# Attention over head pairs: the values product at full array width, and three pauses moved by one or two k-tiles

## The chip, the cores and the metric

The kernel runs on one core of one Trainium2 chip, in one launch. The time is device microseconds of that core. Before the change it is 2374.72 us, the median of three runs (2372.66 to 2375.34). All inputs and the output are float32.

## The reference, cut to what matters

The reference is a chain of two blocks over x of 512 tokens by 2048 features. The change lies in the attention of the first block: sliding-window attention with 32 query heads of 64 features, 4 key/value heads, ALiBi slopes and a sink column.

```
def swa_sink_mixer(h, w_in, sinks):
    q, k, v, z = jnp.split(h @ w_in, [BRANCH, BRANCH + KV_A, BRANCH + 2 * KV_A], axis=-1)
    ...                                   # q: 4 blocks x 128 tokens x 4 kv heads x 8 heads x 64
    kb, vb = band(k), band(v)             # each block of keys with the one before it
    scores = jnp.einsum('bnqhgd,bnkhd->bnhgqk', q, kb) * (HEAD_DIM ** -0.5)
    scores = scores - slopes[:, :, None, None] * dist
    scores = jnp.where(valid[None, :, None, None], scores, NEG)
    p = jax.nn.softmax(jnp.concatenate([scores, sink_col], axis=-1), axis=-1)[..., :-1]
    o = jnp.einsum('bnhgqk,bnkhd->bnqhgd', p, vb).reshape(B, S, BRANCH)
    return o, z
# then y = (o * silu(z)) @ w_out ; x = x + rmsnorm(y)
# second block, two layers: rmsnorm, projections, latent attention, gated convolution,
# attention over 256 memory tokens, gate, output projection, residual
```

## The kernel before

Features lie on the partitions and the 512 tokens on the free axis. A weight chunk is 128 output columns, 1 MB, 16 k-tiles of 128x128. To keep float32 accuracy a weight and an activation are each split in two parts (`hi`, `lo`), and a k-tile is three matmuls of 512 columns (hi·hi, hi·lo, lo·hi), all at line 444 (`passes`, called by `features`). One chunk is thus 48 matmuls. ScalarE makes `hi` (line 748), VectorE `lo` (line 1054).

The first block's attention goes over 16 pairs of heads (`PAIRS`), numbered from 0; both heads of a pair share one key/value head. A pair has two chunks: the query chunk (`chunk1(PAIR1, i)`) and the gate chunk (`chunk1(PAIR1 + 1, i)`). The attention of a pair is laid between k-tiles: `features` takes a list `meanwhile` of (pause, step), and a step runs ahead of the k-tile with the number of its pause. The steps are, on TensorE:

- `scores_first(i)` (lines 519, 520) in the gate chunk of pair i: 16 matmuls of 256 columns into the four banks of `sc`. It waits for `q_split`, the two halves of the query, and for the keys of the pair (`kcur_done`, copies by GpSimd at lines 382 and 386).
- `turn_first(i)` (line 531) in the query chunk of pair i+1: 14 transposes of 128x128 blocks of probabilities. It waits for `probs1`.
- `values_first(i)` (line 543) between the query and the gate chunk of pair i+1: 8 matmuls of the turned probabilities `pt1` (the moving operand, 256 columns, or 128 for the last key block) against the values `vcur` (the stationary operand). It waits for the turned tiles (copied by ScalarE at line 809 and VectorE at line 1193), for `vcur` (GpSimd, line 393) and for the reader of the pair before.

`vcur` holds for each of four key blocks 128 columns: the same 64 value columns twice, once for each head of the pair. Before, the head `par` uses columns `par * 64` on, writes partitions `par * 64` on of the bank `ov[par]`, and the two heads alternate matmul by matmul. The reader (`y_first`, line 1187) takes 64 partitions of each bank.

The query halves that scores wait for are made after the end of the query chunk: VectorE scales the chunk out of PSUM (line 1197, `dg`), ScalarE copies the upper part (line 815), VectorE subtracts (line 1201, two instructions, named `q<-dg,q`), which releases `q_split`. The order on VectorE in one pair is: split of the gate chunk, copies of the turned tiles (1193), scaling (1197), subtraction (1201), `y_first` of the pair before (1187), split of the next query chunk (1054), softmax (1161 to 1178), gate (1207, 1209). Each engine runs its queue in order; a semaphore holds back the instruction that waits and all behind it.

Pair 0 stands alone, pairs 1 to 13 are a hardware loop, and pairs 14 (`A`) and 15 (`B`) are written out behind it: `q_a`, values(13), `q_b` (which is the query chunk of pair 15) with scores(14), `z_a` with turn(14) and the last scores, values(14), `z_b` with turn(15), values(15). Then the activations are split (lines 762 and 1225) and the first block's output product starts.

Of the kernel before, what the change touches and what calls it, by code (L numbers as in the profile page):

```python
# [22 lines left out]
def build(nc, xT, memT, mem, pos, gains, sinks, consts, window, w1, w2, wm, out):  # L23
# [11 lines left out]
    P = 128  # L35
    D, S, MEM = 2048, 512, 256
    KT, TB, MB = D // P, S // P, MEM // P
# [5 lines left out]
    HD, PAIRS, KVH = 64, 16, 4  # L43
    HALVES = (slice(0, HD), slice(HD, 2 * HD))
    PAIR1 = 4
# [32 lines left out]
    def chunk1(p, i=0):  # L78

        new = isinstance(i, int) and i == 0 and p < 2  # L80
        return Chunk(i * 2 + p, p % 2, i + p // 2, None if new else 2)
# [14 lines left out]
    A, B = PAIRS - 2, PAIRS - 1  # L96
    q_a, q_b, z_a, z_b = chunk1(PAIR1, A), chunk1(PAIR1 + 1, A), chunk1(PAIR1, B), chunk1(PAIR1 + 1, B)
# [26 lines left out]
    with ctx:  # L124
        free = [(nc.sbuf_base + 63) // 64 * 64]

        def sb(name, cols, dt=F32, at=None):

            if at is None:
                at = free[0]  # L130
                free[0] += (cols * 4 + 63) // 64 * 64
            return nc.alloc_sbuf_tensor_at(name, [P, cols], dt, offset=at)
# [4 lines left out]
        h_hi, h_lo = sb("h_hi", KT * S, F32R), sb("h_lo", KT * S, F32R)  # L137
# [13 lines left out]
        zt = sb("zt", S, at=free[0])  # L151
# [7 lines left out]
        prob1, pt1 = sb("prob1", 2048, at=m0), sb("pt1", 2048, at=m0 + 8192)  # L159
# [17 lines left out]
        vcur, q1 = sb("vcur", 512, at=a0 + 5120), sb("q1", 2 * S, F32R, at=a0 + 7168)  # L177
# [18 lines left out]
        ov = [ctx.enter_context(nc.psum_tensor(f"ov{s}", [P, 512], F32)) for s in range(2)]  # L196
        sc = ctx.enter_context(nc.psum_tensor("sc", [P, 2048], F32))

        def bank(b, n=512, off=0):
            return sc[:, 512 * b + off:512 * b + off + n]  # L200

        def tile(t, n=S):

            return slice(t * n, (t + 1) * n) if isinstance(t, int) else bass.ds(t * n, n)
# [229 lines left out]
        def _(pe):  # L434
            def begin(c):
                pe.wait_ge(lo_done, c.n + 1)
                if c.back is not None:
                    pe.wait_ge(evacuated[c.slot], c.uses)
# [8 lines left out]
            def k_tile(c, k, x_hi, x_lo, first, last):  # L447
                w, x = tile(k, P), tile(k)
                return passes(acc[c.slot][:, :], hi[c.slot][:, w], lo[c.slot][:, w], x_hi[:, x], x_lo[:, x], first, last)

            def features(c, x_hi, x_lo, ready=None, meanwhile=()):

                begin(c)
                for k in range(KT):
                    for pause, other in meanwhile:
                        if k == pause:
                            other()
                    if ready is not None:
                        ready(k)
                    ins = k_tile(c, k, x_hi, x_lo, k == 0, k == KT - 1)  # L460
                ins.then_inc(chunk_done, 1)
# [37 lines left out]
            def spread(no, to, n=S, diag=dg):  # L499

                pe.wait_ge(diag_done, no + 1)
                pe.matmul(to, ones, diag[:, 0:n], start=True, stop=True).then_inc(r_done, 1)
# [9 lines left out]
            def scores_first(i):  # L512
                pe.wait_ge(q_split, i + 1)
                pe.wait_ge(kcur_done, i * 3 + 3)
                for b in range(TB):
                    for par in range(2):
                        to = bank(2 * par + b // 2, 256, b % 2 * 256)
                        q, k = tile(par * TB + b, P), slice(b * P, b * P + 256)
                        pe.matmul(to, q1[:, q], k_hi[:, k], start=True, stop=False)  # L519
                        ins = pe.matmul(to, q1[:, q], k_lo[:, k], start=False, stop=True)  # L520
                ins.then_inc(scores1, 1)

            def turn_first(i):
                pe.wait_ge(probs1, i + 1)
                for kb in range(TB):
                    for par in range(2):
                        for nxt in range(2):
                            b = kb + nxt
                            if b < TB:
                                src = par * 1024 + b * 256 + (1 - nxt) * P  # L530
                                ins = pe.transpose(bank(kb, P, par * 256 + nxt * P), prob1[:, src:src + P], ident)  # L531
                ins.then_inc(turned1, 1)

            def values_first(i):
                pe.wait_ge(pt1_act, i * 2 + 2)
                pe.wait_ge(pt1_dve, i * 2 + 2)
                pe.wait_ge(vcur_done, i * 2 + 2)
                pe.wait_ge(y1, i + 1)
                for kb in range(TB):
                    n = 256 if kb < TB - 1 else P  # L540
                    for par, rows_ in enumerate(HALVES):
                        src = kb * 512 + par * 256
                        ins = pe.matmul(ov[par][rows_, kb * P:kb * P + n], vcur[:, kb * P + par * HD:kb * P + (par + 1) * HD],  # L543
                                        pt1[:, src:src + n], start=kb == 0, stop=kb == TB - 1, skip_group_check=True)
                ins.then_inc(values1, 1)

            def pair(i, first):

                features(chunk1(PAIR1, i), h_hi, h_lo,
                         meanwhile=[(9, (lambda: spread(1, ov[1][:, 0:MEM], MEM, zt)) if first else lambda: turn_first(i - 1))])  # L550
                if not first:
                    values_first(i - 1)
                features(chunk1(PAIR1 + 1, i), h_hi, h_lo, meanwhile=[(4 if first else 3, lambda: scores_first(i))])

            def last_scores():
                pe.wait_ge(pt1_act, A * 2 + 2)
                pe.wait_ge(pt1_dve, A * 2 + 2)
                scores_first(B)

            pair(0, True)  # L560
            with pe.Fori(1, A) as i:
                pair(i, False)
            features(q_a, h_hi, h_lo, meanwhile=[(9, lambda: turn_first(A - 1))])
            values_first(A - 1)
            features(q_b, h_hi, h_lo, meanwhile=[(3, lambda: scores_first(A))])
            features(z_a, h_hi, h_lo, meanwhile=[(8, lambda: turn_first(A)), (12, last_scores)])
            values_first(A)
            features(z_b, h_hi, h_lo, meanwhile=[(13, lambda: turn_first(B))])
            values_first(B)
# [10 lines left out]
            with pe.Fori(0, LAYERS) as l:  # L580
# [55 lines left out]
                def turn_mem(c):  # L636
                    pe.wait_ge(probs_m, l * MH + (c + 1))
                    for b in range(TB):
                        for k in range(MB):
                            ins = pe.transpose(bank(b, P, k * P), prob_m[:, b * MEM + k * P:b * MEM + (k + 1) * P], ident)  # L640
                    ins.then_inc(turned_m, 1)
# [14 lines left out]
                for c in range(1, MH):  # L656
                    features(chunk2(l, QM + c), h_hi, h_lo,
                             meanwhile=([(2, first_scores)] if c == 1 else []) + [(10 if c == 1 else 8, lambda: turn_mem(c - 1))])
# [919 lines left out]
```

## Time and profile before

| | |
|---|---|
| median of 3 runs | 2374.72 us (2372.66 to 2375.34) |
| profiled execution: time / span | 2374.72 us / 2372.8 us |
| TensorE matmuls (PE) | 2302.9 us busy, 97% of the span |
| weight loads (PEld) | 1860.0 us, 78% |
| VectorE / ScalarE / GpSimd | 46% / 32% / 12% |
| granted TensorE clock, mean | 0.989 |
| chain that ended last | PE 88%, of it line 444 72% |

PE rows are matmuls, PEld rows are weight loads, which can run beside a matmul. A float32 matmul leaves two records (as at lines 543 and 711), an fp32r one leaves one. The recorded length of a matmul is longer than the distance to the next one, since they are pipelined; the distance between two starts is what one costs. Idle time with its releaser stands in brackets at a row's end. The attention of the first block lies between about 68 and 507 us.

### The profile page before, as it was taken

To read this page: it belongs to the slowest core of one execution; us is meant where nothing else is said; L and a number is where in the kernel's file an instruction comes from. 1 tells how busy PE (TensorE), PEld (TensorE's weight loads), DVE (VectorE), ACT (ScalarE), POOL (GpSimd) and SP (SyncE) were. 2 spreads that over 40 slices of the span, in tenths; PEclk is the share of its full clock that TensorE was granted. 3 is DMA by queue.
4 is the path that set the end of the run, shared out by engine and by line. 5 is a ranking of instruction groups with operands and counts; after the bars stand their busy time and mean duration, and the time that the engine had idled before them with its cause. 6 is when DMAs were issued, how large, how long until landed. Compare 5 with 4: busy or idle time off the path is not lost.

```text
span 2372.8 us, 28260 instructions
## 1 busy us (share of the span) xinstructions
PE 2302.9 (97%) x10534; PEld 1860.0 (78%) x10534; DVE 1103.3 (46%) x1410; ACT 757.8 (32%) x1190; POOL 276.4 (12%) x221
## 2 busy tenths in 40 slices
PE   7999999989999999999999999999999999999995
PEld 5888888878885888877877788858888778777884
DVE  7666667662245342444455422443423444554214
ACT  5443343342223221333333322232213333333220
POOL 4111111101124100000000111241000000001113
PEclk9999999999999999999999999999999999999997
DMA  7311222132244222112221322442221122214221
GB/s 280 110 71 71 76 83 79 63 142 106 93 151 182 107 89 106 69 60 76 76 86 42 156 93 106 159 161 107 89 106 69 60 76 76 86 42 160 102 93 71
DMA packets 36357, 238.95 MB, mean 101 GB/s; under 512 B 4160, under 2 KB 4416, under 8 KB 11840
## 3 DMA queue, kind: packets, MB, share of 16 engines
q1 hardware_dynamic: 29520, 204.47, 23.5%
q10 hardware_dynamic: 6336, 25.17, 2.7%
q0 software_dynamic: 432, 8.39, 0.9%
q8 instruction: 43, 0.70, 0.1%
q14 instruction: 26, 0.21, 0.0%
HBM read 221.24 MB, written 16.78 MB: 100 GB/s over the span
## 4 chain that ended last, share of the span: by engine, by line
PE 88%; DVE 5%; issue 2%; ACT 2%; DMA 2%; POOL 1%; ACTq 0%; SPq 0%; DVEq 0%; POOLq 0%
PE acc L444 72%; PE sc L444 4%; PE ov L711 2%; PE sc L597 2%; PE sc L700 1%; DMA xr<-residual 1%; PE ov L543 1%; PE sc L531 1%; DVE g L1086 1%; PE ov L444 1%; PE sc L519 1%; PE sc L692 1%; PE sc L691 1%; DMA g<-xT_dram 1%; PE sc L632 1%
## 5 line engine op out<-in xcount | busy, mean ns | idle before, releaser
L444 PE MATMUL acc<-h_hi,hi 128*128 128x512 f32 x2560 | 1018.4, 398 | 29.3 <-DVE h_lo L1111 16.0
L444 PE MATMUL acc<-h_lo,hi 128*128 128x512 f32 x2560 | 1001.2, 391 | 0.0
L444 PE MATMUL acc<-h_hi,lo 128*128 128x512 f32 x2560 | 1000.9, 391 | 0.0
L1054 DVE TENSOR_TENSOR lo<-raw,hi 128x2048 fp32r<-128x2048 f32 x175 | 388.9, 2222 | 572.2 <-ACT hi L748 569.8
L444 PEld LDWEIGHTS acc<-h_hi,hi 128*128 128x128 f32 x2560 | 483.0, 189 | 138.5 <-issue 20.7
L444 PEld LDWEIGHTS acc<-h_lo,hi 128*128 128x128 f32 x2560 | 483.3, 189 | 102.4 <-issue 5.3
L444 PEld LDWEIGHTS acc<-h_hi,lo 128*128 128x128 f32 x2560 | 482.8, 189 | 101.9
L748 ACT ACTIVATE hi<-raw 128x2048 fp32r<-128x2048 f32 (+2 forms) x178 | 330.8, 1858 | 159.5 <-PE acc L444 145.3
L755 ACT ACTIVATE sq<-acc 128x512 f32<-128x512 f32 x60 | 35.9, 599 | 474.5 <-PE acc L444 474.5
L331 POOL TENSOR_TENSOR sqacc<-sqacc,sq 128x512 f32<-128x512 f32 x74 | 102.0, 1379 | 448.9 <-ACT sq L755 447.1
L408 POOL TENSOR_TENSOR lo<-raw,hi 128x2048 fp32r<-128x2048 f32 x3 | 23.6, 7883 | 1017.8 <-ACT hi L748 1017.8
L821 ACT ACTIVATE prob<-prob,st 128x256 f32<-128x256 f32 x128 | 63.3, 496 | 135.4 <-DVE st L1171 135.4
L1013 ACT ACTIVATE prob<-sc,st 128x512 f32<-128x512 f32 x64 | 43.1, 688 | 87.6 <-DVE st L1439 87.6
L597 PE MATMUL sc<-raw_m,m_n 128*128 128x512 f32 x128 | 58.7, 616 | 0.5 <-DMA raw_m<-wm_dram 0.4
L711 PE MATMUL ov<-prob,v 128*128 128x512 f32 x128 | 57.5, 592 | 0.0
L393 POOL COPY vcur<-vall 128x256 f32 x32 | 19.9, 649 | 297.5 <-PE ov L543 297.2
L1434 DVE SCALAR_TENSOR_TENSOR sq<-sq,acc 128x512 f32<-128x512 f32 x16 | 11.0, 688 | 93.5 <-ACT sq L1008 93.5
L1008 ACT ACTIVATE sq<-acc 128x512 f32<-128x512 f32 x16 | 9.6, 598 | 130.2 <-PE acc L444 130.2
L597 PEld LDWEIGHTS sc<-raw_m,m_n 128*128 128x128 f32 x128 | 25.0, 198 | 31.5 <-issue 30.1
L1438 DVE TENSOR_REDUCE st<-sc 128x4 f32<-128x2048 f32 x16 | 36.7, 2292 | 25.3 <-PE sc L692 25.3
L711 PEld LDWEIGHTS ov<-prob,v 128*128 128x128 f32 x128 | 23.8, 190 | 23.8 <-issue 23.0
L815 ACT ACTIVATE q<-dg 64x512 fp32r<-64x512 f32 x32 | 20.2, 630 | 66.4 <-DVE dg L1197 66.2
(197 smaller groups left out, 2208.4 us busy)
## 6 DMA issues: line engine op xcount, KB each, us to landing
raw<-w_dram SPq DMA_DIRECT2D x162, 1024.0 KB, 4.6
raw_m<-wm_dram SPq DMA_DIRECT2D x16, 1024.0 KB, 6.4
xr<-residual ACTq DMA_DIRECT2D x16, 512.0 KB, 6.2
residual<-g ACTq DMA_DIRECT2D x16, 512.0 KB, 6.1
raw<-w_dram SPq DMA_DIRECT2D x8, 896.0 KB, 4.3
g<-xT_dram SPq DMA_DIRECT2D x4, 1024.0 KB, 12.0
residual<-g POOLq DMA_DIRECT2D x1, 4096.0 KB, 13.8
area<-memT_dram POOLq DMA_DIRECT2D x2, 2048.0 KB, 11.3
```

The source lines that it names most:

```text
L331: pool.tensor_tensor(sqacc[:, :], sqacc[:, :], sq[:, tile(slot)], ALU.add).then_inc(added, 1)
L444: ins = pe.matmul(to, a, b, start=first and n == 0, stop=last and n == 2)
L519: pe.matmul(to, q1[:, q], k_hi[:, k], start=True, stop=False)
L531: ins = pe.transpose(bank(kb, P, par * 256 + nxt * P), prob1[:, src:src + P], ident)
L597: ins = pe.matmul(bank(2 + b), m_n[:, k * MEM + b * P:k * MEM + (b + 1) * P], raw_m[c % 2][:, tile(j)], start=k == 0, stop=k == KT - 1)
L711: ins = pe.matmul(ov[0][:, :], v[:, (2 * k + j) * P:(2 * k + j + 1) * P], prob2[:, tile(k)], start=k == 0, stop=k == TB - 1)
L748: act.activation(hi[c.slot][:, 0:width], raw[c.slot][:, 0:width], ACT.Copy).then_inc(hi_done, 1)
L755: act.activation(sq[:, tile(slot)], src, ACT.Square).then_inc(squared, 1)
L821: act.activation(prob1[:, tile(n, 256)], prob1[:, tile(n, 256)], ACT.Exp, bias=nm[:, n:n + 1], accum_out=ls[:, n:n + 1])
L1013: ins = act.activation(prob2[:, tile(b)], bank(b), ACT.Exp, scale=MLA_SCALE, bias=nm[:, b:b + 1], accum_out=ls[:, b:b + 1])
L1054: dve.tensor_tensor(lo[c.slot][:, 0:width], raw[c.slot][:, 0:width], hi[c.slot][:, 0:width].bitcast(F32), ALU.subtract).then_inc(lo_done, 1)
L1438: link.then(dve.tensor_reduce(mx[:, 0:TB], banks, AX.X, ALU.max))
```

## The change

The values product is written head by head rather than alternating, with both copies of the values as stationary operand (128 columns, and so all 128 partitions of each bank written, of which the reader still takes 64). The turn moves from k-tile 9 to k-tile 8 of the query chunk in pairs 1 to 14 (in pair 0 it is a small broadcast, `spread`, that moves so). The scores move from k-tile 3 to k-tile 1 of the gate chunk in pairs 1 to 14; pair 0 keeps 4. The pauses in `z_a` and `z_b` stay.

```diff
@@ values_first
-                for kb in range(TB):
-                    n = 256 if kb < TB - 1 else P
-                    for par, rows_ in enumerate(HALVES):
+                for par in range(2):
+                    for kb in range(TB):
+                        n = 256 if kb < TB - 1 else P
                         src = kb * 512 + par * 256
-                        ins = pe.matmul(ov[par][rows_, kb * P:kb * P + n], vcur[:, kb * P + par * HD:kb * P + (par + 1) * HD],
-                                        pt1[:, src:src + n], start=kb == 0, stop=kb == TB - 1, skip_group_check=True)
+                        ins = pe.matmul(ov[par][:, kb * P:kb * P + n], vcur[:, tile(kb, P)], pt1[:, src:src + n],
+                                        start=kb == 0, stop=kb == TB - 1, skip_group_check=True)
@@ pair
-                         meanwhile=[(9, (lambda: spread(1, ov[1][:, 0:MEM], MEM, zt)) if first else lambda: turn_first(i - 1))])
+                         meanwhile=[(8, (lambda: spread(1, ov[1][:, 0:MEM], MEM, zt)) if first else lambda: turn_first(i - 1))])
...
-                features(chunk1(PAIR1 + 1, i), h_hi, h_lo, meanwhile=[(4 if first else 3, lambda: scores_first(i))])
+                features(chunk1(PAIR1 + 1, i), h_hi, h_lo, meanwhile=[(4 if first else 1, lambda: scores_first(i))])
@@ q_a and q_b
-            features(q_a, h_hi, h_lo, meanwhile=[(9, lambda: turn_first(A - 1))])
+            features(q_a, h_hi, h_lo, meanwhile=[(8, lambda: turn_first(A - 1))])
...
-            features(q_b, h_hi, h_lo, meanwhile=[(3, lambda: scores_first(A))])
+            features(q_b, h_hi, h_lo, meanwhile=[(1, lambda: scores_first(A))])
```

On TensorE, in the loop over pairs 1 to 13, the turn (line 531) inside the query chunk; a k-tile is three rows of line 444, `hi_51` and `lo_53` are the two parts of the query chunk's weights.

```order
 L444 MATMUL acc<-h_lo,hi_51 128x512
 L444 MATMUL acc<-h_hi,lo_53 128x512
-L444 MATMUL acc<-h_hi,hi_51 128x512
-L444 MATMUL acc<-h_lo,hi_51 128x512
-L444 MATMUL acc<-h_hi,lo_53 128x512
 L531 MATMUL sc<-cst,prob_76 128x128 x14
 L444 MATMUL acc<-h_hi,hi_51 128x512
```

One k-tile of the query chunk that stood ahead of the turn now stands behind it.

On TensorE, in the same loop, the values product (line 543; line 535 is its wait) and the start of the gate chunk, whose weights are `hi_52` and `lo_54`.

```order
 L535 ISA
-L543 MATMUL ov<-pt_77,vcur 64x256 x6
-L543 MATMUL ov<-pt_77,vcur 64x128 x2
+L543 MATMUL ov<-pt_77,vcur 128x256 x3
+L543 MATMUL ov<-pt_77,vcur 128x128
+L543 MATMUL ov<-pt_77,vcur 128x256 x3
+L543 MATMUL ov<-pt_77,vcur 128x128
 L436 REGISTER_ALU
-L444 MATMUL acc<-h_hi,hi_52 128x512
-L444 MATMUL acc<-h_lo,hi_52 128x512
-L444 MATMUL acc<-h_hi,lo_54 128x512
```

The eight matmuls stay eight, in another order and twice as wide; of the three k-tiles between them and the scores two go (this piece shows the first of them), and stand behind the scores instead.

## Rows read from the trace of the kernel before

**Rows 1.** Busy us of PE, PEld, DVE, ACT, POOL in the loop; clock; DMA share; GB/s.

```profile
181.00:454.00 273.00, 273.00 (x1425) 223.65 (x1424) 187.97 (x291) 107.64 (x242) 40.55 (x50) 1.00 0.21 77
```

**Rows 2.** Chain of waits over one pair: start us, length us, what.

```profile
268.85 1.67 PE ov L543 x16
...
272.78 0.25 PE sc L519
...
274.82 14.99 PE acc L444 x66
289.81 1.53 PE sc L531 x14
291.34 4.77 PE acc L444 x21
296.12 1.67 PE ov L543 x16
```

**Rows 3.** Timeline of TensorE around values and scores: start us, length us.

```profile
295.73 0.39 PE L444 MATMUL acc<-h_hi,lo 128*128 128x512 f32 x1
296.05 1.74 PE L543 MATMUL ov<-pt,vcur 128*64 128x256 f32 x16
...
298.05 0.40 PE L444 MATMUL acc<-h_lo,hi 128*128 128x512 f32 x1
...
299.91 0.38 PE L519 MATMUL sc<-k_hi,q 128*128 128x256 f32 x1
```

**Rows 4.** Timeline of TensorE: full-width fp32 products of later stages.

```profile
696.99 2.32 PE L588 MATMUL ov<-m_n,raw_m 128*128 128x256 f32 x10
...
1067.82 0.39 PE L444 MATMUL ov<-m_hi,lo 128*128 128x512 f32 x1
1068.05 3.60 PE L711 MATMUL ov<-prob,v 128*128 128x512 f32 x8
...
1071.71 0.40 PE L444 MATMUL acc<-h_lo,hi 128*128 128x512 f32 x1
...
691.57 1.08 PEld L496 LDWEIGHTS ov<-cst,sqacc 128*128 128x128 f32 x8
```

**Rows 5.** Timeline of the other engines around T, and pair 0.

```profile
296.15 0.69 DVE L1197 SCALAR_TENSOR_TENSOR dg<-acc,sqacc 128x512 f32<-128x512 f32 x1 [0.64 <-PE acc L444]
298.26 1.51 DVE L1201 TENSOR_TENSOR q<-dg,q 64x512 fp32r<-64x512 f32 x2 [1.42 <-ACT q L815]
...
296.96 1.27 ACT L815 ACTIVATE q<-dg 64x512 fp32r<-64x512 f32 x2 [4.00 <-DVE dg L1197]
...
298.03 1.20 POOL L393 COPY vcur<-vall 128x256 f32 x2 [19.67 <-PE ov L543]
...
81.02 1.39 DVE L1201 TENSOR_TENSOR q<-dg,q 64x512 fp32r<-64x512 f32 x2 [1.34 <-ACT q L815]
```

**Rows 6.** Timeline: probabilities, the turn and the turned tiles.

```profile
313.99 2.20 DVE L1178 TENSOR_SCALAR prob<-prob,st 128x256 f32<-128x256 f32 x8
...
316.92 1.69 PE L531 MATMUL sc<-cst,prob 128*128 128x128 f32 x14
...
321.50 1.28 DVE L1193 COPY pt<-sc 128x512 f32<-128x512 f32 x2
```

**Rows 7.** Timeline and chain of waits of the last two pairs.

```profile
484.27 0.36 PE L519 MATMUL sc<-k_hi,q 128*128 128x256 f32 x1
...
486.66 4.49 DMA raw<-w_dram
491.17 1.92 ACT hi L748
...
504.70 1.74 PE L543 MATMUL ov<-pt,vcur 128*64 128x256 f32 x16 [1.02 <-DVE pt L1193]
...
504.63 0.69 DVE L1207 TENSOR_TENSOR zt<-acc,sqacc 128x512 f32<-128x512 f32 x1
```

**Rows 8.** Busy time from 514 to 524 us, columns as in rows 1.

```profile
514.00:524.00 10.00, 6.72 (x19) 5.33 (x20) 8.82 (x10) 2.23 (x5) 3.23 (x2) 0.66 0.30 110
```

## The prediction

> **What bounds the kernel now.** I went first to the granted-clock and busy table of a stretch inside the loop over head pairs. From 181 to 454 us TensorE is busy 273.00 of 273.00 us at full clock, VectorE 188, ScalarE 108, GpSimd 41 [rows 1]. So in this loop every microsecond added to TensorE's queue is a microsecond of the kernel, and nothing that the other engines do counts unless TensorE comes to wait for it. The chain of waits over one pair says the same: it stays on TensorE all the way [rows 2]. One pair runs from one values product to the next, 296.12 - 268.85 = 27.27 us: values 1.67, three k-tiles of the gate chunk (272.78 - 268.85 - 1.67) 2.26, scores 274.82 - 272.78 = 2.04, 22 k-tiles (66 matmuls) 14.99, turning 1.53, seven k-tiles 4.77. A k-tile is 14.99/22 = 0.68 us, a matmul of it 0.227.
>
> **What the values product costs in its two shapes.** Before, it has eight matmuls, each recorded twice (fp32), so 16 records, 12 of 256 moving columns and 4 of 128. They span 1.74 us [rows 3]. A full-width fp32 matmul with 256 moving columns has one record every (2.32 - 0.38)/9 = 0.216 us [rows 4]. At that rate one after another, 16 records would need 12 x 0.216 + 4 x 0.11 = 3.03 us. 1.74 us, with the last record's 0.27 inside it, is about half: the two 64-column halves of the array run at once, one per head, because the loop alternates between them. After, every matmul takes all 128 columns (the array has no second half left) and the heads come one after the other. I take 3.03 us. For the 128-column records 0.11 is half of 0.216, and the weight load does not make it longer by the nearest rows: eight full loads ahead of one-column matmuls took 1.08 us with the last one's 0.19 inside, one every (1.08 - 0.19)/7 = 0.13 us at most [rows 4]. At 0.13 the product would be 3.11.
>
> The narrow shape also pays for its borders. From the last matmul ahead of values (295.73) to the second one behind it (298.05) are 2.32 us [rows 3], where eight shared slots and two ordinary pitches make 6 x 0.216 + 2 x 0.11 + 2 x 0.227 = 1.97: 0.35 us go at the borders. The full-width fp32 product of the later stage has none: its first record starts 0.23 behind the matmul ahead, and the last of its eight, at 1068.05 + 7 x 0.43 = 1071.06 (512 columns, so 2 x 0.216 each), has the second ordinary matmul 0.65 behind it, which is 0.43 + 0.23 [rows 4]. So after, the same distance is 0.23 + 3.03 + 0.23 = 3.49, and TensorE's own work per pair grows by 3.49 - 2.32 = 1.17 us. The Trainium skill, "TensorEngine Tiling (Array Packing)", Key Properties, says that tiles run in parallel and that a change of mode drains TensorE; both directions are in these rows, and the trace adds the size, 0.35 us a product.
>
> **What the moved scores cost.** This is where I expect the number to be decided. Let T be the slot that follows the query chunk's last matmul, 295.73 + 0.23 = 295.96. Scores need the query halves, and these come from a chain on other engines: VectorE scales the chunk (296.15), ScalarE copies (296.96, 1.27 us), VectorE subtracts twice (298.26, 1.51 us, ends 299.77), and scores start at 299.91, 0.14 behind it, or T + 3.95 [rows 3, 5]. Before, TensorE arrives there just as they become ready. Nothing in this chain depends on the values product. After, TensorE arrives at T + 3.03 + 0.68 = T + 3.71, with one k-tile ahead of scores in place of three, and waits. The chain may become a little shorter: GpSimd's copies of vcur follow values and now lie over the subtractions (298.03, 1.20 us); in pair 0, where nothing lies over them, the two took 1.39 us, not 1.51 [rows 5]. After, values end about 1.3 us later, and so do these copies, from about T + 3.4; only the tail of the second subtraction meets them. So scores start between 0.12 earlier than before (T + 3.83) and the same (T + 3.95). I take T + 3.86, near the undisturbed end.
>
> Behind the scores TensorE has two k-tiles more than before: 2 x 0.68 = 1.36 us. Per pair: 1.36 - (3.95 - 3.86) = +1.27 us, bounds 1.24 and 1.36. If the query chain bound nothing it would be 1.17, less up to 0.13 for a weight load that then hides: 1.04. That is the lowest end.
>
> **The turn one k-tile earlier** costs nothing. The normalized probabilities are ready at 313.99 + 2.20 = 316.19, T + 20.23 [rows 6]; TensorE now reaches the turn at 3.86 + 2.04 + 23 x 0.68 = T + 21.5. Before, it came at 316.92 [rows 6], T + 20.96: the slack grows. The turned tiles are copied by VectorE until 321.50 + 1.28 = 322.78, T + 26.82 [rows 6], a place set by VectorE's split before it; values now start at T + 28.5. In pair 0 the spread and the turn move by one tile each and have their inputs.
>
> **How many pairs.** The change is paid between T of pair 1 and T of pair 14: 13 intervals, 13 x 1.27 = 16.5 us.
>
> **The last two pairs** keep their other pauses, and VectorE sets part of their pace. Scores of pair 14 lose their wait; TensorE then is about 1.15 behind its old schedule, and of that the old wait of the last scores for VectorE's copies absorbs 0.2: they start at 485.2 in the old time scale, not 484.27 [rows 7]. The last softmax starts its exponentials only behind a weight split that waited for a DMA (486.66 + 4.49), ending at 491.17 + 1.92 = 493.09 [rows 7], so it is late by 0.3 to 0.4 alone. TensorE adds the wider values(14) (+1.15). It reaches the end of the last gate chunk at 485.2 + 2.04 + 4 x 0.68 + 3.03 + 13 x 0.68 + 1.53 + 3 x 0.68 = 505.4, plus about 0.25 until the last matmul is seen, 505.65. Before, VectorE took that chunk at 504.63, late because of its own queue, and TensorE stood 1.02 us ahead of the last values [rows 7]: that idle time is used up. From there the gate, the split of y and the first output chunk are one chain: +1.0 us (0.6 to 1.4). The last values product itself gets 1.5 us longer beside the split of y, whose last tile comes far behind it.
>
> **Sum.** 16.5 + 1.0 = 17.5 us on the profiled execution's own 2374.72 (span 2372.8), which is also the median: 2392.2 us. One thing can't be placed: in each stage boundary the clock falls to its lower level for a while (0.66 mean over 514 to 524 us [rows 8], 6.8 us at 1.2 GHz). These stretches follow an idle TensorE, and the changed kernel reaches them 17 us later. One more or less of half that length is 1.7 us; I allow 2 us to each side.
>
> **Rivals.**
> 1. The query chain binds nothing and TensorE's own work is all: 13 x 1.04 to 1.17 + 1.0 = 14.5 to 16.2, about 2390. For it: arrival and readiness are only 0.15 apart. Against it: the 0.14 from VectorE's end to scores is in every pair. 9%.
> 2. The full-width weight loads don't hide behind the matmuls once the halves are gone. A load costs 0.11 to 0.13, 16 of them 1.8 to 2.1, so values take 4.9; TensorE reaches scores at T + 5.5, and a pair costs 1.36 + 5.5 - 3.95 = 2.9 more: 13 x 2.9 + 2.8 = 40.5, 2415 us. Against it: the full-width products of the later stage keep a pitch of moving columns alone [rows 4]. 2%. "TensorE: Matmul & The Clock Gate" in the Trainium skill, Part 3, has a sentence that loads overlap running matmuls only where the row group differs; these have the same one. By rows 4 it does not hold for a full-width queue.
> 3. Not slower. The pairing is only how the records look, 64-column matmuls cost as much as full ones, and the array gains the 0.35 us of the borders: 14 x 0.35 = 5 us less, 2370 us. It decides only if the query halves are there by T + 2.3, since otherwise scores wait as above, and the rows have them at T + 3.81. Or the extra work lies in idle time of TensorE: rows 1 leave none. 2%, half of it within 0.2%.
> The forecast has 87%.
>
> The range holds the forecast's bounds (16.1 + 0.6 to 17.7 + 1.4) with the clock's 2 us, and most of rival 1: 2389.3 to 2395.6. A measurement of this kernel tells about 0.2% (4.7 us) from no change. Faster by more than that 0.01, within 0.02, slower 0.97.
>
> **What would show it.** In the profile after, a pair takes 28.5 us; values records are 128 columns wide, 16 of them over 3.0 to 3.3 us, with no gap at the border; the first scores matmul starts 3.8 to 3.95 us behind T with TensorE or its weight load waiting for VectorE's subtractions, and this wait has a row of its own in the list of waits; the turn waits for nothing; the 1.02 us wait of the last values is gone. A pair of 28.3 us without that wait would be rival 1, values over 4 us rival 2, a pair near 27.3 rival 3. Gains or losses behind 540 us other than by stretches at the low clock would make the reasoning incomplete.

## The result and the profile after

The changed kernel takes 2389.77 us (median of 4 runs, 2385.26 to 2390.73); the kernel before, in all its runs of this comparison, 2373.69 us. The ratio is 1.0065, with a 95% interval of 1.0048 to 1.0084: slower by 15.4 us by the ratio (16.1 by the medians), of which the interval leaves 11 to 20. The forecast was 2392.2 us with 2389.3 to 2395.6. The median lies 0.5 us above the low end, the ratio on 2373.69 us gives 2389.1, 0.2 below it. The direction held, the size was forecast too large by 2.4 to 3.1 us. The profiled execution took 2389.51 us with a span of 2387.6 us, 14.8 more than before.

One pair of the loop in the chain of waits after (start us, length us, what), against [rows 2]:

```profile
305.04 3.03 PE ov L543 x16
308.07 0.70 PE acc L444 x3
308.77 0.31 PE sc L519
...
310.87 15.67 PE acc L444 x69
326.54 1.53 PE sc L531 x14
328.07 5.47 PE acc L444 x24
```

In this view the chain still never leaves TensorE; a wait of about 0.1 us ahead of the scores, which it does not show, is read from the timeline below. Values went from 1.67 to 3.03 us, the k-tiles ahead of the scores from 2.26 to 0.70, the k-tiles between scores and turn from 14.99 to 15.67, and those behind the turn from 4.77 to 5.47.

TensorE's timeline at the same place (start us, length us), against [rows 3], and the weight load of the first scores matmul:

```profile
304.65 0.39 PE L444 MATMUL acc<-h_hi,lo 128*128 128x512 f32 x1
304.88 3.19 PE L543 MATMUL ov<-pt,vcur 128*128 128x256 f32 x16
...
308.14 0.40 PE L444 MATMUL acc<-h_lo,hi 128*128 128x512 f32 x1
308.38 0.40 PE L444 MATMUL acc<-h_hi,lo 128*128 128x512 f32 x1
308.70 0.38 PE L519 MATMUL sc<-k_hi,q 128*128 128x256 f32 x1
...
333.38 3.19 PE L543 MATMUL ov<-pt,vcur 128*128 128x256 f32 x16
```

```profile
308.69 0.19 PEld L519 LDWEIGHTS sc<-k_hi,q 128*128 128x128 f32 x1 [0.36 <-issue]
```

A pair takes 333.38 - 304.88 = 28.50 us, where it took 27.27. The borders are gone: values start 0.23 behind the matmul ahead, the ordinary pitch, and from that matmul to the second one behind the product are 308.14 - 304.65 = 3.49 us, as forecast. The slot T is 304.88 here, and scores start at 308.70 = T + 3.82. Their ordinary slot would have been 308.38 + 0.23 = 308.61.

The other engines between T and the scores (VectorE, then GpSimd), against [rows 5]:

```profile
305.07 0.69 DVE L1197 SCALAR_TENSOR_TENSOR dg<-acc,sqacc 128x512 f32<-128x512 f32 x1 [2.00 <-PE acc L444]
307.18 1.39 DVE L1201 TENSOR_TENSOR q<-dg,q 64x512 fp32r<-64x512 f32 x2 [1.41 <-ACT q L815]
```

```profile
308.31 0.85 POOL L393 COPY vcur<-vall 128x256 f32 x2 [22.40 <-PE ov L543]
```

The subtractions took 1.51 us while GpSimd copied beside them; they take 1.39 us now that the copies start at T + 3.43, only 0.26 us ahead of the subtractions' end (307.18 + 1.39 = 308.57). The copies got shorter too, 0.85 us for the two instead of 1.20. The scores start 0.13 behind the subtractions' end, where it was 0.14 before.

The end of the last gate chunk on VectorE (its brackets: idle, and who ended it), against the 504.63 of [rows 7]:

```profile
519.83 1.29 DVE L1193 COPY pt<-sc 128x512 f32<-128x512 f32 x2 [0.20 <-PE sc L531]
521.90 0.69 DVE L1207 TENSOR_TENSOR zt<-acc,sqacc 128x512 f32<-128x512 f32 x1 [0.78 <-PE acc L444]
...
540.10 0.69 DVE L1225 TENSOR_TENSOR h_lo<-g,h_hi 128x512 fp32r<-128x512 f32 x1 [0.70 <-ACT h_hi L762]
```

VectorE now waits for TensorE there, where TensorE had waited 1.02 us for VectorE. The gate starts 521.90 - 504.63 = 17.27 us later. The last split of y, at 522.84 before, starts at 540.10: 17.26 us later. Up to this point the forecast was 17.5.

### The profile page after: what moved, and what is told of

Read it like the earlier page. It is cut to its first block, busy times and chain, and to the rows that moved or that the text cites. A ratio compares the mean times of both kernels' runs of the same rounds, so it can differ in the third digit from the quotient of the medians.

```text
span 2387.6 us, 28260 instructions
## 1 busy us (share of the span) xinstructions
PE 2319.8 (97%) x10534; PEld 1884.8 (79%) x10534; DVE 1100.9 (46%) x1410; ACT 759.7 (32%) x1190; POOL 273.5 (11%) x221
## 4 chain that ended last, share of the span: by engine, by line
PE 90%; DVE 4%; issue 2%; DMA 1%; ACT 1%; POOL 1%; ACTq 0%; SPq 0%; DVEq 0%; POOLq 0%
PE acc L444 73%; PE sc L444 4%; PE ov L711 2%; PE ov L543 2%; PE sc L597 2%; PE sc L700 1%; PE sc L531 1%; DVE g L1086 1%; PE ov L444 1%; PE sc L519 1%; DMA xr<-residual 1%; PE sc L520 1%; PE sc L691 1%; PE sc L692 1%; DMA g<-xT_dram 1%
## 5 line engine op out<-in xcount | busy, mean ns | idle before, releaser
L444 PE MATMUL acc<-h_hi,hi 128*128 128x512 f32 x2560 | 1016.1, 397 | 28.3 <-DVE h_lo L1111 16.0
L543 PE MATMUL ov<-pt,vcur 128*128 128x256 f32 (+1 forms) x256 | 51.1, 353 | 0.0
L543 PEld LDWEIGHTS ov<-pt,vcur 128*128 128x128 f32 x256 | 46.0, 190 | 6.2
## 6 DMA issues: line engine op xcount, KB each, us to landing
area<-memT_dram POOLq DMA_DIRECT2D x2, 2048.0 KB, 11.4
```

The costliest lines, as they stand in the source:

```text
L444: ins = pe.matmul(to, a, b, start=first and n == 0, stop=last and n == 2)
L543: ins = pe.matmul(ov[par][:, kb * P:kb * P + n], vcur[:, tile(kb, P)], pt1[:, src:src + n], start=kb == 0, stop=kb == TB - 1, skip_group_c ...
```

## The experiments

Every time is device microseconds. Experiments 1 to 4 are compared with the same 17 runs of the kernel before (median 2374.06). The pair time is the distance between two values products eight pairs into the loop.

**1. The wide product with the old pauses** (from the changed kernel):

```diff
-[(8, ... turn_first(i - 1))]   (1, lambda: scores_first(i))
+[(9, ... turn_first(i - 1))]   (3, lambda: scores_first(i))
```

> The wide values product alone, with the turn at 9 and the scores at 3 as before. My theory: TensorE's own work is all there is, since at k-tile 3 it comes to the scores at T + 3.03 + 3 x 0.68 = T + 5.1, long behind the query halves (T + 3.7); the first scores weight load then hides, which saves up to 0.13. A pair takes 27.27 + 1.17 - 0.13 = 28.3 us, 0.2 less than in the changed kernel (28.50); over 13 pairs 2.5 us less. Rival, the width is all and the moved pauses are neutral: 28.50. Rival, the moved scores are all: 27.27.

Measured: ratio 1.0056 (1.0042 to 1.0070), median 2386.63. Two values products of neighbouring pairs, 28.33 us apart:

```profile
302.48 3.19 PE L543 MATMUL ov<-pt,vcur 128*128 128x256 f32 x16
...
330.81 3.19 PE L543 MATMUL ov<-pt,vcur 128*128 128x256 f32 x16
```

As my theory had it. The width by itself costs 1.06 us a pair, and with the wide product the moved pauses cost another 0.17: TensorE then reaches the scores just too early. In whole-kernel time this kernel and the changed one can't be told apart (the intervals overlap); in the traces they can.

**2. The narrow product with the new pauses** (from the kernel before):

```diff
-[(9, ... turn_first(i - 1))]   (3, lambda: scores_first(i))
+[(8, ... turn_first(i - 1))]   (1, lambda: scores_first(i))
```

> The moved pauses alone (8 and 1), with the narrow alternating values product. My theory: TensorE comes to the scores at T + 2.4 and waits until T + 3.95; two k-tiles stand behind instead of ahead: a pair takes 27.27 + 1.36 = 28.63 us, as much as or more than with the wide product, and the list of waits has about 1.4 us per pair of TensorE for VectorE's subtraction. GpSimd's vcur copies lie over the subtractions as before, so these take 1.51 us; if GpSimd is not what made them 1.39 in the changed kernel, a pair takes 28.50. Rival, the width is all: near 27.3.

Measured: ratio 1.0079 (1.0065 to 1.0093), median 2390.70. TensorE, then VectorE, then the first row of TensorE's list of waits (us in total, times, longest):

```profile
305.54 1.73 PE L543 MATMUL ov<-pt,vcur 128*64 128x256 f32 x16
309.41 0.38 PE L519 MATMUL sc<-k_hi,q 128*128 128x256 f32 x1 [1.24 <-DVE q L1201]
...
334.16 1.73 PE L543 MATMUL ov<-pt,vcur 128*64 128x256 f32 x16
```

```profile
307.76 1.51 DVE L1201 TENSOR_TENSOR q<-dg,q 64x512 fp32r<-64x512 f32 x2 [1.42 <-ACT q L815]
```

```profile
PE sc L519 <- DVE q L1201: 18.1, 15, 1.2
```

28.62 us a pair. The moved pauses alone cost 1.35 us, more than the whole change (1.23), though the products (1.73 us) and the subtractions (1.51) are as long as before. The parts don't add: 1.06 + 1.35 = 2.41, together 1.23, because the wide product fills the time in which the scores would wait. This is the test of the step that decided the forecast, that the query chain and not TensorE sets the start of the scores: they start 0.14 behind the subtractions' end here (307.76 + 1.51 = 309.27) too, however early TensorE comes. The subtractions take 1.51 us here, with GpSimd's copies over them as before.

**3. The narrow product, head by head** (from the kernel before):

```diff
-for kb in range(TB):
-    for par, rows_ in enumerate(HALVES):
+for par, rows_ in enumerate(HALVES):
+    for kb in range(TB):
```

> The narrow product (64 columns) with the heads one after the other, pauses as before. My theory: only neighbours in different halves of the array run at once, so the 16 records run singly (3.0 us) and the borders still cost 0.35: a pair takes 27.27 + 1.5, less up to 0.13 for the scores' hidden load, 28.65 us. Rival, the cost of a matmul goes by its stationary columns and not by its neighbour: 27.27.

Measured: ratio 1.0052 (1.0038 to 1.0065), median 2385.46. TensorE, and the weight loads:

```profile
301.50 0.39 PE L444 MATMUL acc<-h_hi,lo 128*128 128x512 f32 x1
301.81 2.65 PE L543 MATMUL ov<-pt,vcur 128*64 128x256 f32 x16
...
304.73 0.39 PE L444 MATMUL acc<-h_lo,hi 128*128 128x512 f32 x1
```

```profile
301.81 2.41 PEld L543 LDWEIGHTS ov<-pt,vcur 128*64 128x64 f32 x16 [0.35 <-issue]
```

A pair takes 28.07 us (the next product starts at 329.88). Both expectations missed: not 27.27, so the order does make the pairing, and not 28.65. The product spans 2.65 us, where fully single records would take 12 x 0.216 + 4 x 0.11 less the last pitch plus its 0.27, 3.19 as in the wide product. 0.54 us are saved. In the single records of one such product, read one by one from the trace (first start 273.75) the second head's first matmul starts at 274.67, with the fifth of the first head's eight records (274.66), and the first head's last one starts only at 275.20. So the halves pair across a short stretch of the queue, here three to four records, and not only with the neighbour. The borders cost their 0.3 here too: from 301.50 to 304.73 are 3.23 us, 0.91 more than the 2.32 of before, and the product alone is 2.65 - 1.74 = 0.91 longer. The pair grows by 0.80; TensorE comes later to the scores, whose first load now hides, as in experiment 4.

**4. The kernel before with the scores one k-tile later:**

```diff
-(4 if first else 3, lambda: scores_first(i))   [(3, lambda: scores_first(A))]
+(4 if first else 4, lambda: scores_first(i))   [(4, lambda: scores_first(A))]
```

> The kernel before with the scores one k-tile later (4, not 3) in pairs 1 to 14. My theory: before, the scores' first weight load starts only 0.14 us behind the subtraction and lies bare; one k-tile later it hides, and the softmax behind has room (its first instruction waits for VectorE, 1.5 us behind the scores). A pair takes 27.27 - 0.13 = 27.14 us, 1.8 us less over 14 pairs. Rival, the margin at the scores costs nothing: 27.27.

Measured: ratio 0.9997 (0.9988 to 1.0006), median 2372.53 of 11 runs.

```profile
295.34 1.74 PE L543 MATMUL ov<-pt,vcur 128*64 128x256 f32 x16
...
299.62 0.39 PE L444 MATMUL acc<-h_hi,lo 128*128 128x512 f32 x1
299.85 0.28 PE L519 MATMUL sc<-k_hi,q 128*128 128x256 f32 x1
...
322.47 1.74 PE L543 MATMUL ov<-pt,vcur 128*64 128x256 f32 x16
```

27.13 us a pair, as expected: scores start one ordinary pitch (0.23) behind the matmul ahead, their record is 0.28 long, not 0.38, since the load lies beside it. The 1.8 us are in the trace and are too few to show in the whole time. This is the best version I found, and it can't be told from the kernel before.

**5. The wide product with the heads alternating** (from the changed kernel, the two loops swapped back):

> The changed kernel with the two heads alternating again, at full width. My theory: with 128 columns no two matmuls share the array, so the order says nothing: values span 2.92 us from first to last start, a pair takes 28.50 us as in the changed kernel. Rival, the order by head also costs: under 28.5, towards 27.3.

Measured: one run, 2387.41 us.

```profile
304.39 3.19 PE L543 MATMUL ov<-pt,vcur 128*128 128x256 f32 x16
...
332.89 3.19 PE L543 MATMUL ov<-pt,vcur 128*128 128x256 f32 x16
```

28.50 us a pair, the same as in the changed kernel. At full width the order says nothing; the cost is that of the width.

**6 to 8. Both kernels again**, unchanged, one run each:

> The kernel before once more, to see how far the stages behind the first block's attention vary in one and the same program. In the profile of before they took 1849.9 us from the last split of y (522.84) to the end, in the changed kernel 1847.4, in four variants 1845.7 to 1849.0. My theory: this differs only by which stretches at the lower clock fall where, so before also gives 1845 to 1850, and its pair stays at 27.27. Rival, the change shortens the later stages: before stays at 1849.9 +- 0.5.

> The changed kernel once more. My theory: pair 28.50, the last split of y at 540.1, and 1845 to 1850 us behind it, with other stretches at the lower clock. Rival, the change shortens the later stages: 1847.4 +- 0.5.

> As r1: pair 27.27, and 1845 to 1850 us behind the last split of y if the lower clock's stretches make the spread; 1849.9 +- 0.5 if the change made it.

Measured: 2374.07, 2390.27 and 2375.82 us; one more run of the kernel before, without a trace, took 2371.16. The pair took 27.26, 28.50 and 27.26 us, and the last split of y started at 523.24, 540.03 and 523.30: up to here both programs repeat to 0.5 us. Behind it they don't. The seven different programs are the same instruction by instruction from there on. The low clock is the granted clock's lower level, summed from 500 us to the end of the span, so that the stretch that lies across the last split is in it. TensorE also waits there for the DMA of weights (`raw_m`, lines 588 and 597, in two places of the kernel):

| kernel | from the last split of y to the end, us | at the low clock from 500 us on, us | TensorE waits for `raw_m`, us |
|---|---|---|---|
| before / again / again | 1849.9 / 1848.9 / 1850.5 | 51.8 / 42.1 / 52.3 | 0.5 / 2.9 / 1.2 |
| changed / again | 1847.4 / 1848.3 | 45.1 / 45.6 | 0.8 / 0.8 |
| exp. 1 / 2 / 3 | 1849.0 / 1846.2 / 1846.1 | 45.2 / 42.2 / 38.8 | 2.1 / 0.6 / 1.8 |
| exp. 4 / 5 | 1845.7 / 1845.8 | 38.4 / 37.8 | 2.3 / 1.7 |

(The lengths are cut to a tenth.) The spread is 4.8 us in equal code. It goes with both columns: a fit over the ten profiles, an estimate from this table, gives 0.4 us per us at the low clock and 1.0 us per us of waiting, and meets every row within 0.7 us. The clock alone does not explain it. The second run of before and experiment 2 have equal low clock (42.1 and 42.2) and differ by 2.7 us; these are their rows in the list of waits (us in total, times, longest):

```profile
PE sc L597 <- DMA raw_m<-wm_dram: 2.9, 2, 1.6
```

```profile
PE sc L597 <- DMA raw_m<-wm_dram: 0.6, 2, 0.4
```

About the same two stretches of code in the kernel before, the changed one (with a third stretch ahead of them) and experiment 4 (stretch, us, then busy us (count) of PE, PEld, DVE, ACT, POOL, granted clock, DMA share, GB/s):

```profile
1025.00:1035.00 10.00, 8.70 (x43) 7.05 (x42) 2.77 (x2) 1.86 (x6) 0.00 (x0) 0.83 0.15 41
1345.00:1357.00 12.00, 9.10 (x29) 6.93 (x28) 5.95 (x2) 3.19 (x4) 4.02 (x2) 0.72 0.64 250
```

```profile
740.00:760.00 20.00, 16.69 (x42) 7.51 (x41) 8.21 (x19) 4.23 (x8) 7.34 (x6) 0.91 0.58 205
1045.00:1052.00 7.00, 5.70 (x37) 4.96 (x36) 2.29 (x1) 1.41 (x5) 0.00 (x0) 1.00 0.19 59
1362.00:1376.00 14.00, 11.11 (x50) 8.87 (x49) 7.40 (x5) 3.52 (x4) 5.81 (x2) 1.00 0.56 215
```

```profile
1025.00:1035.00 10.00, 8.70 (x48) 6.82 (x47) 4.32 (x5) 2.30 (x6) 0.00 (x0) 1.00 0.15 41
1345.00:1357.00 12.00, 9.77 (x43) 8.10 (x44) 4.47 (x2) 2.89 (x3) 2.19 (x2) 1.00 0.77 292
```

Before, the clock falls to half for part of both (mean 0.83 and 0.72); in the changed kernel it stays full there and falls once at another place (0.91 over 740 to 760 us); in experiment 4, which is the kernel before but for one pause, both stay full. Each stretch at the low clock between 500 and 2200 us, in all ten profiles, begins during or just behind an idle time of TensorE of 1.3 to 4.1 us, but not every such idle time brings one: TensorE is busy for 8.70 of the same 10 us in the kernel before and in experiment 4 above. Whether the changed kernel's later part is shorter on average stays open: two executions (1847.4, 1848.3) against three (1848.9 to 1850.5) lean that way by 2 us, and the fit puts all of it down to less low clock and less waiting in these two. Whether the change brings that about or chance does, no run shows. By the whole times such an effect of a moved stage is small, if there is one: in experiments 1 to 4 the last split of y starts 13.6, 17.7, 10.7 and -1.5 us later than in the mean of the three profiles of before, and the median times differ by 12.6, 16.6, 11.4 and -1.5 us.

## Where the forecast's size was off, and what of its mechanism held

- **TensorE bounds the loop.** Right: it waits for no more than about 0.1 us in a pair, and each pair's added time reached the end of the stage unchanged.
- **The narrow product runs its two halves at once, the wide one can't.** Right: 3.03 us forecast for values, 3.03 in the chain. Experiment 3 shows that the pairing depends on the order, experiment 5 that at full width the order says nothing.
- **The borders, 0.35 us.** Right: 3.49 us from the last matmul ahead of the wide product to the second one behind it, forecast 3.49, leave nothing for them.
- **The query chain sets the start of the scores.** Right: T + 3.86 forecast (3.83 to 3.95), T + 3.82 measured. The scores start 0.13 to 0.14 behind the subtractions' end in every kernel whose scores wait (before, changed, experiments 2 and 5). The subtractions are longer where GpSimd's copies lie over them: 1.39 us where the copies meet only their last quarter microsecond (changed kernel, experiments 1 and 5), 1.51 to 1.52 with the copies over them (before, experiment 2), 1.62 in experiment 3, where the copies start together with the second subtraction. The forecast took 0.09 of the 0.12 us; all of it came. 1.23 us a pair, just under the forecast's 1.24 to 1.36: over 13 pairs 16.0, not 16.5.
- **A wait for VectorE with a row of its own.** Wrong: there is no such row. The wait is about 0.1 us (308.70 against the slot at 308.61), and it shows only in the first load, which has 0.36 us of idle time put down to issue, since the matmul ahead is recorded until 308.78, past the start of the scores. The pair time told rival 1 from the forecast (28.33 in experiment 1, 28.50 here), the list of waits did not.
- **The last two pairs, +1.0 us.** Right: 17.27 at the last gate, less 13 x 1.23 and 0.27 by which pair 0 started later in this execution, leaves 1.0.
- **The clock and the base.** This is the step that failed, in size: "One more or less of half that length is 1.7 us; I allow 2 us to each side", on top of a base of 2374.72 us, and nothing else for the part behind the stage. The stage came out 17.3 us longer and the whole profiled execution only 14.8, because the part behind it was 2.5 us shorter. The runs show two things in place of "one more or less". The low clock there came to 37.8 to 52.3 us in ten profiles, a spread of four stretches of 3.4 us (51.8 in the base, 45.1 in the changed kernel). And TensorE's waits for the DMA of `raw_m`, which the sum put at nothing, took 0.5 to 2.9 us. The forecast had named as a sign that it is incomplete any gain or loss behind 540 us other than by the low clock, and this is one. Together they move that part by 4.8 us in the same code.
- **Luck in the base.** Single runs of the kernel before lie between 2369.9 and 2377.6 us, and 2374.72 was 1.0 above the comparison's median and 0.7 above that of the 17 runs. Of the 3.1 us between 2392.2 and 2389.1, 1.0 is thus the base and 0.5 the pair; the rest, about 1.6, can only be the part behind the stage and the scatter of the runs. With 2374.06 and 3 to 4 us of margin the range would have been some 2387 to 2397. The stated range is also 0.1 to 0.2 off its own terms, which give 2389.4 to 2395.8.

Of the rivals, 1 (the chain binds nothing, about 2390) names the time that was measured better than the forecast does, but only by the part behind the stage: its pair of 28.3 us describes experiment 1 and not the changed kernel; 2 (loads don't hide) fell with the 3.03 us of the values; 3 (not slower) fell with the ratio.

## What to carry to other kernels

Matmuls that use half of the array's columns are worth writing in alternation on different halves, since the same number of full-width ones took 3.03 us here instead of 1.67, even though the borders between the shapes cost some 0.3 us. A pause in a hand-written order is a matched pair with the length of what stands ahead of it: before moving one, work out when its inputs are ready from the engines that make them, since two k-tiles on the wrong side cost their full time in each turn of the loop (1.35 of 1.36 us), and one k-tile more of margin hid a weight load (0.14 us). When the effect is under a per cent, compare the stage in the traces, and take the base and the spread of the rest from several executions.

## What the runs showed that I had not expected

Two halves of the array pair up across three to four records of the queue: head by head, the narrow product still took 2.65 us and not 3.19. VectorE's two subtractions were 0.12 to 0.23 us longer with GpSimd's copies over them (1.51 and 1.62, against 1.39); what that costs the kernel before was not measured by itself. And the later stages, with the same instructions in all ten profiles, differed by up to 4.8 us with how long the clock was at 1.2 GHz and how long TensorE waited for the weights of `raw_m`.
